# Pairs of 32-token experts in one block, in a two-layer transformer on one Trainium2 core

## The reference

```
scores = sigmoid(x @ router_w)             # 256 tokens, 16 experts in 4 groups of 4
# the best group by its two best biased scores; the two best experts in it; their scores, normed, are gates
for e in range(16):
    he = silu(x @ wg[e]) * (x @ wu[e])     # 1024 -> 512
    y += gates[:, e:e+1] * (he @ wd[e])    # 512 -> 1024
```

## Time and profile before

| | before |
|---|---|
| time of a run, median of 3 | 1230.95 us (1230.71 to 1235.37) |
| the profiled execution: its own time, and its span | 1234.19 us, 1232.3 us |
| mean granted clock of TensorE | 0.925 of full |
| PE busy | 1046.5 us (85%) |
| DVE, ACT, POOL busy | 347.8, 225.8, 138.9 us |
| read by the weight queue | 291.42 MB |
| mixture of layer 0, from its first product to its last combine | 271.1 to 531.5 us |
| mixture of layer 1, the same | 936.8 to 1201.4 us |

### The profile page before, as it was taken

The page is one execution under the profiler, slowest core; times in us unless marked ns, Lnnn a source line. Parts: engine busy times, 40 slices in busy tenths (PEclk is TensorE's granted clock), DMA queues, the critical chain, the costliest instruction groups (busy, mean ns, idle before and its releaser), DMA issues. The chain is left out here.

```text
span 1232.3 us, 14417 instructions
## 1 busy us (share of the span) xinstructions
PE 1046.5 (85%) x5784; PEld 609.2 (49%) x5784; DVE 347.8 (28%) x818; ACT 225.8 (18%) x527; POOL 138.9 (11%) x159
## 2 busy tenths in 40 slices
PE   4899997969989988769999867677877998989874
PEld 1344476743433433248786567577753343333343
DVE  0101153272010101043334166677246000101012
ACT  1200252122110101022333311210031211011112
POOL 1000000010000000010000065663010000000001
PEclk9799997979999999789999979799888999999886
DMA  9976750539779898973764300100153878989840
GB/s 381 428 304 270 308 208 1 213 130 366 304 313 425 341 430 353 432 311 137 274 221 189 137 1 4 65 1 1 69 204 128 334 291 373 425 348 427 343 200 34
DMA packets 22157, 299.54 MB, mean 243 GB/s; under 512 B 2560, under 2 KB 2688, under 8 KB 4032
## 3 DMA queue, kind: packets, MB, share of 16 engines
q1 hardware_dynamic: 20304, 291.42, 58.4%
q0 software_dynamic: 1776, 7.08, 1.5%
HBM read 295.34 MB, written 3.15 MB: 242 GB/s over the span
## 5 line engine op out<-in xcount | busy, mean ns | idle before, releaser
L507 PE MATMUL bank<-ring,arena 128*64 128x512 f32 x640 | 142.5, 596 | 9.1 <-DMA ring<-slots 7.6
L515 PE MATMUL bank<-ring,arena 128*32 128x512 f32 x576 | 80.8, 698 | 36.8 <-DMA ring<-slots 34.2
L968 PE MATMUL bank<-act_t,ring 128*128 128x256 f32 x384 | 91.5, 394 | 7.2 <-POOLq L277 7.2
L507 PEld LDWEIGHTS bank<-ring,arena 128*64 128x64 f32 x640 | 45.6, 137 | 93.8 <-issue 83.9
L1479 PE MATMUL bank<-ring,act_t 128*128 128x512 f32 x192 | 87.8, 612 | 3.9 <-ACTq L277 3.9
L968 PEld LDWEIGHTS bank<-act_t,ring 128*128 128x128 f32 x384 | 74.1, 198 | 21.7 <-POOLq L277 7.6
L552 PE MATMUL bank<-arena 64*128 64x256 f32 x608 | 78.6, 399 | 1.2 <-DVEq L440 1.2
L832 DVE COPY arena<-bank 128x256 f32<-128x256 f32 x38 | 16.1, 424 | 222.3 <-PE bank L448 222.3
L536 PE MATMUL bank<-ring,arena 128*64 128x512 f32 x320 | 73.1, 598 | 1.9 <-ACT arena L658 1.9
L895 POOL COPY arena<-arena 128x256 f32 (+1 forms) x34 | 17.0, 501 | 444.5 <-PE bank L507 199.5
L305 PE MATMUL bank<-ring,par 128*32 128x512 f32 x384 | 51.9, 663 | 15.2 <-DMA ring<-slots 14.1
(11 more groups left out here) (325 smaller groups left out, 1387.2 us busy)
## 6 DMA issues: line engine op xcount, KB each, us to landing
ring<-slots SPq DMA_DIRECT2D x138, 2048.0 KB, 11.8
cst<-consts SPq DMA_DIRECT2D x1, 1276.5 KB, 31.9
act_t<-x_t POOLq DMA_DIRECT2D x1, 1024.0 KB, 12.4
act_t<-state POOLq DMA_DIRECT2D x1, 1024.0 KB, 7.5
out_st<-arena POOLq DMA_DIRECT2D x4, 256.0 KB, 2.8
out_y<-arena POOLq DMA_DIRECT2D x2, 512.0 KB, 3.4
par<-params SPq DMA_DIRECT2D x1, 613.0 KB, 3.9
arena<-nat_bias POOLq DMA_DIRECT2D x1, 512.0 KB, 20.2
```

Source lines behind the costliest of these rows:

```text
L507: last = pe.matmul(bk[64 * t:64 * t + 64, :], x[:, 4 * m + c, 0:64], w[:, c, 512 * t:512 * t + 512], start=(m == 0 and c == 0), stop=(m == ...
L515: last = pe.matmul(bk[at:at + 32, :], x[:, 4 * m + c, 0:32], w[:, c, 512 * t:512 * t + 512], start=(m == 0 and q == 0), stop=(m == 1 and q ...
L968: last = pe.matmul(bank[i % 3][:, 0:T], w[:, c, (i % 4) * P:(i % 4 + 1) * P], act_t[:, c, :], start=(c == 0), stop=(c == KC - 1))
```

## The change

Two ranks of at most 32 tokens form one block of 64 columns of tokens, and each keeps 32 of them. Gate and up, and down, run for such a pair in four column tiles: two output halves for each of the two experts, over the whole contraction. Nothing is left to be folded, so `fold32` and the whole path of 32-token blocks are gone. Rank 7 becomes a single block of 64. LEAN has eleven blocks of 64 and four pairs, fifteen in a layer. The order is that of `UNITS`; the slots of a pair come interleaved, m = 0 of both, m = 1 of both, m = 2 of both (`SEQ`). The transposes of `pick` go ahead of down, into the bank that gate and up have left, in place of bank 2. The buffer of m = 2 is freed before the copy to `yb` and not after it. SP reads the expert's row at each position. POOL makes two copies for a pair, each with a `value_load`.

```diff
-TURNS = (0, 1, 7, 2, 8, 5, 9, 3, 10, 6, 11, 4, 12, 13, 14, 15)
-LEAN_CAP = (64, 64) + (128,) * 3 + (64,) * 2 + (32,) * 9
+UNITS = ((0,), (1,), (8, 9), (2,), (5,), (10, 11), (3,), (6,), (12, 13), (4,), (7,), (14, 15))
+SEQ = [(r, m) for unit in UNITS for m in range(3) for r in unit]
+LEAN_CAP = (64, 64) + (128,) * 3 + (64,) * 3 + (32,) * 8
...
+            def gate_up(parts, x, bk, final):
+                wide = 64 // len(parts)
                 for m in range(2):
+                    ws = []
+                    for r, at in parts:
+                        k = wait_slot(pe, n0, SEQ.index((r, m)))
+                        ws.append(ring[:, k, :].rearrange("p (c n) -> p c n", c=4))
+                    for c in range(4):
+                        for e, w in enumerate(ws):
                             for t in range(2):
+                                to = 64 * t + wide * e
+                                last = pe.matmul(bk[to:to + wide, :], x[:, 4 * m + c, wide * e:wide * e + wide],
+                                                 w[:, c, 512 * t:512 * t + 512],
                                                  start=(m == 0 and c == 0), stop=(m == 1 and c == 3))
+                            if m == 0 and c == 3 and final:
+                                last.then_inc(slot_free[slot_of(n0, parts[e][0], 0)], 1)
                 return last
...
+            def down(parts):
+                wide = 64 // len(parts)
+                ws = []
+                for r, at in parts:
+                    k = wait_slot(pe, n0, SEQ.index((r, 2)))
+                    ws.append(ring[:, k, :].rearrange("p (f n) -> p f n", f=FC))
+                for f in range(FC):
+                    col = (f % 2) * P + (f // 2) * 64
+                    for e, w in enumerate(ws):
                         for t in range(2):
+                            to = 64 * t + wide * e
+                            last = pe.matmul(bank[3][to:to + wide, :], ht[:, col + wide * e:col + wide * e + wide],
+                                             w[:, f, 512 * t:512 * t + 512], start=(f == 0), stop=(f == FC - 1))
                 return last
...
+            def outputs(plan, n):
+                nb = block_count(L, n)
+                pe.wait_ge(S("pick_ready"), nb)
                 if n >= 1:
                     pe.wait_ge(S("gates_moved"), nb - 1)
+                for s_ in range(2):
+                    last = pe.transpose(bank[n % 2][:, s_ * P:(s_ + 1) * P], pick[:, s_, :], ident)
+                last.then_inc(S("gt_done"), 1)
+                pe.wait_ge(S("hid_copied"), nb)
                 if n >= 1:
                     pe.wait_ge(S("y_copied"), nb - 1)
+                down(plan[n]).then_inc(S("y_done"), 1)
...
                 for n in range(2, len(plan) + 2):
                     if n < len(plan):
-                        nb = block_count(L, n)
-                        pe.wait_ge(S("xe_ready"), nb)
-                        pe.wait_ge(S("gu_read"), nb - 2)
-                        pe.wait_ge(S("he_ready"), nb - 2)
+                        pe.wait_ge(S("xe_ready"), block_count(L, n))
+                        pe.wait_ge(S("gates_moved"), block_count(L, n - 2))
                         products(plan, n)
...
                 act.wait_ge(S("y_done"), nb)
+                if last_of_rank(plan, n):
+                    for r, at in plan[n]:
+                        act.sem_inc(slot_free[slot_of(n0, r, 2)], 1)
                 act.activation(yb[:, n % 2, :], bank[3][:, :], ACT.Copy).then_inc(S("y_copied"), 1)
-                if last_of_rank(plan, n):
-                    act.sem_inc(slot_free[at_ring(n0, 3 * i + 2)[0]], 1)
...
+                    for e, (r, j) in enumerate(parts):
+                        at = pool.value_load(flags[0:1, 1, r:r + 1], min_val=0, max_val=2 * T + (2 * 64 if plan is LEAN else 0))
+                        if n >= 2 and e == 0:
+                            pool.wait_ge(S("gu_done"), block_count(L, n - 2))
+                        last = pool.tensor_copy(xe[:, n % 2, :, wide * e:wide * e + wide], xg[:, :, bass.ds(at + j, wide)])
+                    last.then_inc(S("xe_ready"), 1)
...
+                    r, m = SEQ[pos - n0]
+                    if pos == n0 + 3 * len(FIXED):
                         sp.wait_ge(S("turns_ready"), layer + 1)
+                    if r < len(FIXED):
+                        at = 3 * FIXED[r]
+                    else:
+                        at = sp.value_load(flags[0:1, 0, r:r + 1], min_val=0, max_val=3 * N_EXP - 3)
                     row = at + (n0 + m)
                 sp.wait_ge(slot_free[k], pos // RING)
```

More of the change, by code:

```diff
@@ L428, in last_of_rank, with slot_of @@
         def last_of_rank(plan, n):
[L429 removed]
+            return n + 1 == len(plan) or plan[n + 1][0][0] != plan[n][-1][0]
+        def slot_of(n0, r, m):
+            return at_ring(n0, SEQ.index((r, m)))[0]
         def either(eng, layer, signals, body, again=None):
@@ L517, in gate_up @@
-                    if m == 0 and final:
-                        last.then_inc(slot_free[k], 1)
-                return last
[L521 to L534, removed]
-                        for t in range(2):
[L536 to L545, removed]
+                            if m == 0 and c == 3 and final:
+                                last.then_inc(slot_free[slot_of(n0, parts[e][0], 0)], 1)
@@ L558, in products, with combined @@
             def products(plan, n):
-                i, r, at, wide = plan[n]
                 x = xg[:, :, 64 * n:64 * n + 64] if n == 0 or (n == 1 and plan is LEAN) else xe[:, n % 2]
-                gate_up(i, x, bank[n % 2], wide, n > 0 and last_of_rank(plan, n)).then_inc(S("gu_done"), 1)
+                gate_up(plan[n], x, bank[n % 2], n > 0 and last_of_rank(plan, n)).then_inc(S("gu_done"), 1)
             def turned(plan, n):
-                wide = plan[n][3]
                 nb = block_count(L, n)
-                pe.wait_ge(S("he_ready" if wide == 64 else "gu_read"), nb)
+                pe.wait_ge(S("he_ready"), nb)
+                transposes(pe, bank[2], [hb[:, n % 2, j * P:(j + 1) * P] for j in range(2)]).then_inc(S("hid_done"), 1)
+            def outputs(plan, n):
+                nb = block_count(L, n)
+                pe.wait_ge(S("pick_ready"), nb)
                 if n >= 1:
                     pe.wait_ge(S("gates_moved"), nb - 1)
-                hidden(n, wide).then_inc(S("hid_done"), 1)
-            def outputs(plan, n):
-                i, r, at, wide = plan[n]
-                nb = block_count(L, n)
-                pe.wait_ge(S("hid_copied" if wide == 64 else "he_ready"), nb)
+                for s_ in range(2):
+                    last = pe.transpose(bank[n % 2][:, s_ * P:(s_ + 1) * P], pick[:, s_, :], ident)
+                last.then_inc(S("gt_done"), 1)
+                pe.wait_ge(S("hid_copied"), nb)
                 if n >= 1:
                     pe.wait_ge(S("y_copied"), nb - 1)
-                down(i, wide).then_inc(S("y_done"), 1)
-                pe.wait_ge(S("pick_ready"), nb)
-                transposes(pe, bank[2], [pick[:, s_, :] for s_ in range(2)]).then_inc(S("gt_done"), 1)
+                down(plan[n]).then_inc(S("y_done"), 1)
+            def combined(plan, n):
+                nb = block_count(L, n)
+                pe.wait_ge(S("y_copied"), nb)
+                pe.wait_ge(S("gates_moved"), nb)
+                combine(n % 2, n == 0, n + 1 == len(plan))
             def experts(plan):
@@ L603, in experts @@
                         turned(plan, n - 1)
[L604 to L607, removed]
+                    combined(plan, n - 2)
                     if 3 <= n <= len(plan):
@@ L853, in experts @@
                 for n in range(1, len(plan) + 1):
-                    if n >= 3 and plan[n - 1][3] == 32:
-                        product(plan, n - 1)
-                    if 2 <= n < len(plan) and plan[n][3] == 64:
+                    if 2 <= n < len(plan):
                         product(plan, n)
@@ L886, in experts @@
             def experts(plan):
-                for n, (i, r, j, wide) in enumerate(plan):
+                for n, parts in enumerate(plan):
                     if n == 0 or (n == 1 and plan is LEAN):
@@ L890, in experts @@
                         continue
[L891 to L895 removed]
+                    wide = 64 // len(parts)
+                    if n == 2 or (n == 1 and plan is FULL):
+                        pool.wait_ge(S("xg_copied"), 12 * L + (10 if plan is LEAN else 12))
+                    for e, (r, j) in enumerate(parts):
[4 more added lines that the diff above has]
+                    last.then_inc(S("xe_ready"), 1)
             either(pool, L, ("xe_ready",), experts)
```

81 lines of the change are left out of this document (20 added, 61 removed).

## The result

The changed kernel takes 1308.67 us (median of 4, 1303.59 to 1309.27), the kernel before 1233.16 us with the runs taken beside it. The ratio is 1.060, 95% interval 1.055 to 1.0645: slower by about 75 us, and the interval is far from 1. The forecast was 1297 with a range of 1270 to 1322. The profiled execution had 1303.59 us and a span of 1301.8.

What follows compares the result with a forecast made beforehand. The prediction took the six-buffer ring to bound the kernel. Less PE work, longer waits and lower clock gave +34.4 and +32.2 us in the two layers; 1230.95 + 66.6 = 1297.5, stated as 1297, range 1270 to 1322.

Steps and rivals of the forecast that it cites:

- What bounds the kernel: Mixtures before the change: DMA and PE nearly level, the six-buffer ring decides; 20.9 us of weight waits a layer.
- PE's work: Both mixtures: pairs and rank 7's larger block bring a layer's TensorE work to 215.7 us, 13.7 less than before.
- The term for POOL: First pair of a layer: PE waits for two token copies with a `value_load` between, +0.7 us.
- The ring: Pairs and next ranks wait for late-freed buffers, 9.4 and 12.9 us at a time; 66.1 us a layer for 20.9.
- The 0.2 for the release: Estimated us between a down product's end, which frees a buffer, and the issue of the transfer into it.
- the waits of 1.4: PE idles 1.4 us for a rank's second gate and up slot, such as 3.1, after its first half.
- The clock: After long waits TensorE runs at 1.2 GHz for a time: 2.3 us each, 11.0 us a layer.
- The sum: Layer mixtures: work, waits, clock and 2 us of rest give 294.8 and 296.8 us, +66.6 over both.
- the ledger: Prediction's list of when buffers come free and slots land, 7.8 us to landing, 4.9 between slots.
- The one that ended faster: Rival: TensorE's work decides, transfers stay hidden, layer waits under 34.6 us; 1203.6 us, chance 0.05.
- The one in which the clock stays low through most of the work: Rival: pairs and their next halves run at 1.2 GHz; above 1322, to 1340 us, chance 0.04.
- The one in which the tiles don't run at once: Rival: a pair's four column tiles serialize, 7.0 + 3.6 us more per pair; 1297 to 1380 us, chance 0.01.

Runs made afterwards that it cites:

- order of use: Transfers of a mixture asked for as slots are used and freed: changed kernel so ordered 1203.56 us, kernel before so ordered 1192.74 us.
- fitting it to the pairs: Changed kernel, a pair's down slots split around the next unit's gate slots, and POOL loading both offsets before its wait: 1180.02 us, ratio 0.954.

## Why the prediction was right, and where its size was off

**What bounds the kernel.** Right: neither engine but the ring. Before, an order of use takes 40 us off with the same work and bytes.

**PE's work.** Right in its sign and roughly in size: the pairs save 20 to 23 us for the 27.4 of the sum. The kernel with pairs cut to a quarter of its bytes needed 217.1 us in layer 1, against 217.7 (215.7 and 1.95); the kernel before, cut likewise, needed 229.9 and 230.9, against 229.4 and 231.4. The pause of 1.9 us in layer 0 was put at nothing. The term for POOL was too small, 0.7 where it was 1.3: in the kernel after PE waited 2.56 us for the first pair's tokens and not 1.30, because the first `value_load` now stands behind POOL's wait as well, not only the second between the copies. With both loads ahead of the wait PE waited 1.64.

**The ring.** Right in place and in size: 9.47 and 12.89 us in the rows above for 9.4 and 12.9; over both layers the six are 9.19 to 9.75 and the four 12.89 to 13.08. The sum of the waits is 124.5 us for 132.2. Most of the difference, 7.5, lies in the waits of 1.4 behind a slow half, which the slow half hides; the rest in the last down product. The 0.2 for the release, an estimate, came out as 0.24: SP issues at 373.93, behind a down product that ends at 373.69. The transfer landing after 7.8 us was the right price. The Trainium skill, page "DMA: Bandwidth & Descriptors", section "Anatomy of one DMA", gives 2.0 us and the bytes at 436 GB/s, by its figures an estimate of 6.8, but for transfers that GpSimd issues; these are SyncE's, and with 6.8 each turnaround would have come out 1 us short of these rows.

**The clock.** Right in place, too large in size: 22 us by the sum, 16.7 in the mixtures of the kernel that keeps TensorE busy. The halves after the long waits took 5.3 to 6.4 us for 3.64 in the pairs, 1.7 to 2.8 more. Over all twelve long waits the products behind them took 23.0 us more, 1.9 each, where the sum had 2.3; the two halves behind rank 2's waits of 2.80 and 2.60 us took 1.7 more each, and the sum had nothing for them. The Trainium skill, page "TensorE: Matmul & The Clock Gate", section "HAM oscillation — how this bites in real kernels", says that an engine which waits for a transfer at each step starts each step at the lower clock. The trace agrees, with the 5.98 us after 9.47 idle above.

**The sum.** For the two mixtures it was +34.4 and +32.2, and the profile has +34.8 and +31.2: 66.6 for 66.0. That it fits to 0.6 is partly luck. The waits were 7.7 us under the ledger, and against that stood 4.4 of lower clock (26.4 in the rows for 22), 1.9 for the pause and 1.2 for POOL. The part that is not luck is the hidden waits of 1.4: the sum had 5.6 of them in the waits and took the same 5.6 off the clock. The whole kernel's median grew by 75.5, so about 9 us were not in the sum. Of the profiled execution's 69.5, 3.5 are in code that nobody touched; the three other executions are 5 us longer still, at a mean clock of 0.886 to 0.895 against its 0.906. That this is the clock again, outside and inside the mixtures, is argued from these means, not shown. The forecast ratio of 1.054 lies just under the interval of 1.055 to 1.0645.

**The rivals.** The one that ended faster needed a layer's waits under 34.6 us; they were 62. That its condition was the right one is shown by the order of use, which brings the waits to 15 and the time below the kernel before. The one in which the clock stays low through most of the work had 1322 and more; both mixtures had a granted clock of 0.88, and the down products between the waits took 3.64 and 3.65 us, as at the full clock before. The one in which the tiles don't run at once fell with the 3.64 us of a pair's half.

## What to carry to other kernels

In a ring that one queue fills in order, write down for each position when the buffer six positions earlier comes free and when its own data are wanted; an early slot whose buffer comes free late holds up all behind it, and a better grouping of the work can lose more there than it saves. Ask for transfers in the order of use and release, which here was worth 40 us without the pairs and 105 with them, for little more than a changed constant; fitting it to the pairs brought 24 more, some 1.8 of them POOL's. Merging small pieces makes each demand on the ring larger (six buffers of six here), so the order has to be settled anew after it. And a forecast that fits should be taken apart term by term: here four terms were off by 1 to 8 us, and their sum by 0.6.

## What the runs showed of the hardware

The clock of TensorE differs between executions in code that is the same. Windows of attention, ahead of the first mixture, in the kernel before and then in the kernel after:

```profile
157.00:185.00 28.00, 27.19 (x206) 19.97 (x207) 13.98 (x51) 14.93 (x56) 0.00 (x0) 1.00 0.54 202
```

```profile
160.00:193.00 33.00, 32.59 (x205) 22.64 (x203) 13.06 (x48) 14.29 (x53) 0.00 (x0) 0.80 0.44 166
```

The same 206 and 205 matmuls took 28 us at a clock of 1.00 and 33 at 0.80, though PE was busy nearly all of both. The first product of the first mixture, ahead of which all ten kernels here do the same work, began between 271.1 and 281.7 us in their profiled executions: 271.1, 273.4 and 278.1 without pairs, 271.7 to 281.7 with them. So a profile's span differs by up to 10 us here by nothing that was changed, and a change is better read from the window that it touches.

Idle TensorE can also be kept at its clock with matmuls that nobody reads: ten of them, 8.85 us, brought the half behind them from 5.98 to 3.64 us.
